# A hybrid decoder layer: FFN up-projection by seven Strassen products per value/gate pair, down-projection in groups of 4 k tiles between the pairs

## The reference, cut to what matters

```python
def conv_ffn(xn, buf, w_up, cw, cb, w_down):        # xn: 576 tokens used x 1024
    up = xn @ w_up                                   # 1024 x 5632: value half, gate half
    upc, new_buf = causal_dwconv(up, buf, cw, cb)    # width 3, along the tokens
    val, gate = jnp.split(upc, 2, axis=-1)
    return (jax.nn.gelu(gate) * val) @ w_down, new_buf   # 2816 x 1024

x = x + merged @ w_out
x = x + conv_ffn(rms_norm(x, norm2_g), ...)[0]
```

## Time and profile before

| | |
|---|---|
| median of 3 runs | 1052.52 us (1052.02 to 1055.92) |
| span of the profiled execution | 1050.4 us |
| mean granted TensorE clock | 0.997 |
| 19513 instructions, of them matmuls | 7952 |

### The profile page before, as it was taken

The page is one execution under the profiler, slowest core; times in us unless marked ns, Lnnn a source line. Parts: engine busy times, 40 slices in busy tenths (PEclk is TensorE's granted clock), DMA queues, the critical chain, the costliest instruction groups (busy, mean ns, idle before and its releaser), DMA issues.

```text
span 1050.4 us, 19513 instructions
## 1 busy us (share of the span) xinstructions
PE 1037.5 (99%) x7952; PEld 1015.8 (97%) x7952; DVE 697.8 (66%) x1046; ACT 403.3 (38%) x593; POOL 369.7 (35%) x178
## 2 busy tenths in 40 slices
PE   8999999999999999999999999999999999999996
PEld 7899999999999999999999999999999999999996
DVE  6787558946656477474735769999930289999423
ACT  7567786314434433432522343222221122222432
POOL 4333334342322223222133344333433333344430
PEclk9999999999999999999999999999999999999998
DMA  8533332468486786874552223223332222323355
GB/s 215 172 87 94 102 93 69 108 177 222 106 246 172 157 256 146 221 186 138 178 179 82 81 80 101 81 84 90 96 97 77 61 81 86 91 86 101 93 101 169
DMA packets 262748, 132.90 MB, mean 127 GB/s; under 512 B 82208, under 2 KB 256533, under 8 KB 262408
## 3 DMA queue, kind: packets, MB, share of 16 engines
q1 hardware_dynamic: 262454, 131.63, 45.7%
q10 hardware_dynamic: 210, 0.07, 0.0%
HBM read 104.17 MB, written 25.29 MB: 123 GB/s over the span
## 4 chain that ended last, share of the span: by engine, by line
PE 93%; issue 3%; DVE 1%; POOL 1%; ACT 0%; DMA 0%; DVEq 0%; SPq 0%; POOLq 0%; ACTq 0%
PE ring L2307 44%; PE ring L2717 23%; PE bank L2717 17%; PE bank L2549 2%; PE bank L2353 1%; POOL wlo L1029 1%; PE bank L2532 1%; PE bank L2629 1%; PE bank L2460 1%; PE bank L2617 1%; DMA x_tok<-in_x_prompt 0%; DVE x_split L1903 0%; PE ring L2340 0%; PE bank L2568 0%; PE bank L2588 0%
## 5 line engine op out<-in xcount | busy, mean ns | idle before, releaser
L2307 PE MATMUL ring<-x_split,whi 128*128 128x322 f32 (+2 forms) x1952 | 347.6, 300 | 0.1
L1029 POOL TENSOR_TENSOR wlo<-stage,whi 128x1024 fp32r<-128x1024 f32 x78 | 196.9, 2526 | 398.0 <-ACT whi L1088 398.0
L2307 PEld LDWEIGHTS ring<-x_split,whi 128*128 128x128 f32 x1952 | 294.5, 189 | 8.9 <-issue 8.1
L2307 PE MATMUL ring<-x_split,wlo 128*128 128x256 f32 (+1 forms) x976 | 210.4, 297 | 0.0
L2307 PEld LDWEIGHTS ring<-x_split,wlo 128*128 128x128 f32 x976 | 164.6, 189 | 0.0
L1088 ACT ACTIVATE whi<-stage 128x1024 fp32r<-128x1024 f32 x79 | 83.3, 1054 | 81.3 <-PE ring L2307 69.6
L1073 POOL TENSOR_TENSOR wlo<-stage,whi 128x1024 fp32r<-128x1024 f32 x28 | 71.8, 2565 | 108.1 <-ACT whi L1463 108.1
L2717 PE MATMUL ring<-x_split,whi 128*128 128x256 f32 (+1 forms) x512 | 88.7, 295 | 0.0
L1578 DVE SCALAR_TENSOR_TENSOR conv<-up,cols,conv 128x592 f32<-128x592 f32 x88 | 75.5, 858 | 3.1
L2717 PEld LDWEIGHTS ring<-x_split,whi 128*128 128x128 f32 x512 | 77.0, 189 | 0.0
L2208 DVE TENSOR_SCALAR conv<-up,cols 128x592 f32<-128x592 f32 x44 | 72.2, 1641 | 3.1
(11 more groups left out here) (403 smaller groups left out, 2112.6 us busy)
## 6 DMA issues: line engine op xcount, KB each, us to landing
stage<-in_w_in SPq DMA_DIRECT2D x56, 512.0 KB, 4.2
stage<-in_w_up SPq DMA_DIRECT2D x44, 512.0 KB, 3.8
stage<-in_w_down SPq DMA_DIRECT2D x16, 704.0 KB, 4.5
stage<-in_w_branch_a SPq DMA_DIRECT2D x8, 512.0 KB, 3.8
c_sample<-in_state_mlstm_C SPq DMA_DIRECT2D x16, 256.0 KB, 6.9
out_s_mlstm_C<-c_sample SPq DMA_DIRECT2D x16, 256.0 KB, 2.4
stage<-in_w_branch_b SPq DMA_DIRECT2D x8, 512.0 KB, 3.9
stage<-in_w_out SPq DMA_DIRECT2D x8, 512.0 KB, 3.7
```

Source lines behind the costliest of these rows:

```text
L1029: pool.tensor_tensor(spaced(wlo[:, slot]), packed(stage[:, slot, 0:n]), spaced(whi[:, slot]).bitcast(F32), ALU.subtract).then_inc(w_lo, 1)
L2307: last = pe.matmul(of(z, t0 or -2, t1), w[:, kk * WS:kk * WS + P], x_, start=kk == 0 and m == 0, stop=kk == kn - 1 and m == 2)
```

## The change

It does the up-projection of a value/gate pair as a 2 x 2 block product: blocks over the k halves (4 k tiles each), value and gate, and two token parts of 290 columns that overlap by two. Seven block products (`B11`, `B21`, `B22`, `T1` to `T4`) take the place of eight. Four of them (`T1`, `T2`, `T3`, `B22`) use sums of x blocks and four (`T1` to `T4`) sums of weight quarters; x sums are formed once, in the w_out stage, by ACT and DVE, and their high and low parts kept (`fxh`, `fxl`, seven operands); the weight sums are formed for each pair by DVE in place (`weight_sums`, `weight_sum_two`, `weight_sum_four`), 512 elements per partition each. Products that several results need are accumulated in one bank and copied out in between by ACT (`first_part`, `second_part`, `third_part`); DVE adds the copies to what is in PSUM and scales them into `up`.

A weight piece is now a quarter or a sum of quarters (512 elements) and goes through a ring of 7 slots of high and low parts; ACT rounds piece n + 7 after TensorE has used piece n, POOL subtracts. The first tap goes from DVE to ACT; the history copy becomes a max of an operand with itself.

The down-projection goes in groups of 4 k tiles (the last has 2), accumulated in `resid`: two of the 8 tiles of a group stand between the products of a pair, from pair 5 on; the last two groups come behind the pairs, in one accumulation. Evictions of down tiles rise from 16 to 40. Several semaphores that fire once are merged, and the last stores of the convolution's rows move behind the other stores.

```diff
+GROUP, LAG, GROUPS = 4, 5, 6
+RING = 7
...
+def down_at(i):
+    g, step = divmod(i - LAG, GROUP)
+    return (g, 2 * step) if 0 <= g < GROUPS - 2 and i < NPAIR else None
...
+def weight_order():
+    for i in range(NPAIR):
+        d = down_at(i)
+        yield "B11", i
+        yield "B21", i
+        if i:
+            yield "T4", i - 1
+        if d:
+            yield "D", *d
+        yield "T2", i
+        if i:
+            yield "B22", i - 1
+        yield "T1", i
+        if d:
+            yield "D", d[0], d[1] + 1
...
+        def down_out(g, m):
+            if g < GROUPS - 2:
+                return wide[1]
+            return (wide[1], bank2(0), wide[0], bank2(1))[m % 4 if m < 7 else 0]
...
+            def load_pair(i):
+                if i >= 2:
+                    sp.wait_ge(piece_split, split_done("B22", i - 2))
+                for q0, c0 in ((0, P * i), (2, FF + P * i)):
+                    sp.dma_start(fst[i % 2][:, q0:q0 + 2].rearrange("p q (k m) -> p (q k) m", m=P),
+                                 w_up.rearrange("(k p) m -> p k m", p=P)[:, :, c0:c0 + P]).then_inc(pair_loaded[i % 2], 16)
...
+            for n, key in enumerate(PIECES):
+                pool.wait_ge(piece_rounded, rounded(*key))
+                pool.tensor_tensor(in_blocks(flo[n % RING], key), packed(piece(key)),
+                                   in_blocks(fhi[n % RING], key).bitcast(F32), ALU.subtract).then_inc(piece_split, 1)
...
+                    act.wait_ge(t_done, 4 * i + SUM_AT[op])
+                else:
+                    act.wait_ge(pair_loaded[i % 2], pair_in(i))
+                if n >= RING:
+                    act.wait_ge(tile_done, unit_done(*PIECES[n - RING]))
+                act.activation(in_blocks(fhi[n % RING], key), packed(piece(key)), ACT.Copy).then_inc(piece_rounded, 1)
...
+            def ahead(*key):
+                if UNIT[key] + RING < len(PIECES):
+                    piece_hi(UNIT[key] + RING)
...
+            def first_tap(i, j):
+                ft = i + UPT // 2 * j
+                act.wait_ge(up_ready, 2 * i + j + 1)
+                if i:
+                    act.wait_ge(prod_done, i)
+                act.activation(cv[:, j, 0:CV_N], up[:, j, 0:CV_N], ACT.Identity,
+                               scale=cols[:, C_FCW[0] + ft:C_FCW[0] + ft + 1], bias=cols[:, C_FCB + ft:C_FCB + ft + 1]
+                               ).then_inc(tap_done, 1)
...
+            for i in range(NPAIR):
+                d = down_at(i)
+                first_part(i)
+                ahead("B11", i)
+                ahead("B21", i)
+                if i:
+                    ahead("T4", i - 1)
+                if i >= 2:
+                    product_hi(i - 2)
+                if d:
+                    ahead("D", *d)
+                second_part(i)
+                if i:
+                    first_tap(i - 1, 0)
+                ahead("T2", i)
+                if i:
+                    ahead("B22", i - 1)
+                ahead("T1", i)
+                if i:
+                    first_tap(i - 1, 1)
+                if d:
+                    ahead("D", d[0], d[1] + 1)
+                third_part(i)
+                ahead("T3", i)
+                if i:
+                    gelu(i - 1)
+            def square(m):
+                act.wait_ge(tile_evicted, down_out_count(FINAL + m + 1))
+                if m >= 3:
+                    act.wait_ge(fin_acc, m - 2)
...
+            def weight_sums(i):
+                dve.wait_ge(pair_loaded[i % 2], pair_in(i))
+                w = fst[i % 2]
+                tt(w[:, 4], w[:, 3], w[:, 2], ALU.subtract).then_inc(t_done, 1)
+                tt(w[:, 2], w[:, 2], w[:, 0], ALU.subtract).then_inc(t_done, 1)
+            def weight_sum_two(i):
+                w = fst[i % 2]
+                dve.wait_ge(t_done, 4 * i + 2)
+                dve.wait_ge(piece_split, split_done("B11", i))
+                tt(w[:, 0], w[:, 2], w[:, 3], ALU.subtract).then_inc(t_done, 1)
+            def weight_sum_four(i):
+                w = fst[i % 2]
+                dve.wait_ge(t_done, 4 * i + 3)
+                dve.wait_ge(piece_split, split_done("B21", i))
+                tt(w[:, 1], w[:, 1], w[:, 0], ALU.add).then_inc(t_done, 1)
...
+            def x_low(op, k, in_, f=None):
+                dve.wait_ge(x2_hi, x_count(op, k))
+                if f is None:
+                    tt(fxl[op][:, k], in_, fxh[op][:, k].bitcast(F32), ALU.subtract).then_inc(x2_lo, 1)
+                else:
+                    mul_add(fxl[op][:, k], in_, gain(f), fxh[op][:, k].bitcast(F32), ALU.mult, ALU.subtract).then_inc(x2_lo, 1)
...
+                if f < QK:
+                    tt(xdiff[:, :], one, two, ALU.subtract).then_inc(x2_sum, 1)
+                    x_low("B11", k_, one, f)
+                    x_low("T3", k_, xdiff[:, :], f)
+                else:
+                    n = QK + 3 * k_
+                    dve.wait_ge(x2_hi, x_count("T3", k_))
+                    mul_add(xsum[:, k_], two, gain(f), xsum[:, k_]).then_inc(x2_sum, 1)
+                    dve.wait_ge(x2_sum, n + 1)
+                    mul_add(xdiff[:, :], halves_of(k_)[0], gain(k_), xsum[:, k_], ALU.mult, ALU.subtract).then_inc(x2_sum, 1)
+                    dve.wait_ge(x2_sum, n + 2)
+                    mul_add(xfour[:, :], one, gain(f), xdiff[:, :]).then_inc(x2_sum, 1)
+                    x_low("B21", k_, one, f)
+                    x_low("T1", k_, xsum[:, k_])
+                    x_low("T2", k_, xdiff[:, :])
+                    x_low("T4", k_, two, f)
+                    dve.wait_ge(x2_sum, n + 3)
...
+            def last_rows(i, j):
...
+                ft, U = i + UPT // 2 * j, up[:, j]
+                h_ = hist[:, :, ft:ft + UPT + 1:UPT]
+                st(tt(sample_rows(U)[:, :, 0:FW - 1], h_, h_, ALU.max))
+                st.wait()
+                cpy(flast[:, ft].rearrange("p (b l) -> p b l", l=2),
+                    grouped(U[:, US0 - 2:UW_F - 2], UG)[:, :, 0:2]).then_inc(up_ready, 1)
...
+            def first_sum(i):
+                dve.wait_ge(part_copied, parts(i, 1))
+                dve.wait_ge(tile_done, unit_done("B21", i))
+                tt(s_one[:, 0:QS], s_one[:, 0:QS], acc(i, 1)[:, 0:QS], ALU.add).then_inc(c11_added, 1)
...
+            def third_scaled(i):
+                z = acc(i, 0)
+                dve.wait_ge(tile_done, unit_done("T4", i))
+                dve.wait_ge(c11_scaled, i + 1)
+                st(tt(up[:, 0, QS:US0], z[:, 0:UH_F], rtwo[:, 0:UH_F], ALU.mult))
+                tt(sample_rows(up[:, 0])[:, :, FW - 1:], grouped(z[:, UH_F:QT], LS), grouped(rtwo[:, UH_F:QT], LS), ALU.mult
+                   ).then_inc(c21_scaled, 1)
+                last_rows(i, 0)
+            def second_sum(i):
+                s_ = s_two[i % 2]
+                dve.wait_ge(part_copied, parts(i, 2))
+                dve.wait_ge(tile_done, unit_done("B22", i))
+                tt(s_[:, 0:QS], s_[:, 0:QS], acc(i, 2)[:, 0:QS], ALU.add).then_inc(c12_added, 1)
+                dve.wait_ge(c12_added, i + 1)
+                st(tt(up[:, 1, 0:QS], s_[:, 0:QS], rbc[:, 0:QS], ALU.mult))
+                last_rows(i, 1)
...
+            def fourth_sum(i):
+                dve.wait_ge(part_copied, parts(i, 3))
+                dve.wait_ge(tile_done, unit_done("T1", i))
+                tt(s_three[:, :], s_three[:, :], acc(i, 2)[:, 0:QT], ALU.add).then_inc(c22_added, 1)
...
+            def other_taps(i, j):
+                ft, U, c_ = i + UPT // 2 * j, up[:, j], cv[:, j, 0:CV_N]
+                w = [cols[:, C_FCW[m] + ft:C_FCW[m] + ft + 1] for m in range(FW)]
+                dve.wait_ge(tap_done, 2 * i + j + 1)
+                st.link(mul_add(c_, U[:, 1:1 + CV_N], w[1], c_))
+                ins = mul_add(c_, U[:, 2:2 + CV_N], w[2], c_)
...
+            def down_evict(g, m):
+                dve.wait_ge(tile_done, unit_done("D", g, m))
+                tt(resid[:, m, META:], of_down(down_out(g, m), META), resid[:, m, META:], ALU.add).then_inc(tile_evicted, 1)
+            for i in range(NPAIR):
+                d = down_at(i)
+                if i >= 2:
+                    product(i - 2)
+                if i:
+                    third_scaled(i - 1)
+                else:
...
+                first_sum(i)
+                if i >= 2:
+                    product_lo(i - 2)
+                if i + 1 < NPAIR:
+                    weight_sums(i + 1)
+                if i:
+                    other_taps(i - 1, 0)
+                first_scaled(i)
+                if i + 1 < NPAIR:
+                    weight_sum_two(i + 1)
+                if d:
+                    down_evict(*d)
+                if i:
+                    second_sum(i - 1)
+                if i + 1 < NPAIR:
+                    weight_sum_four(i + 1)
+                if i:
+                    other_taps(i - 1, 1)
+                if d:
+                    down_evict(d[0], d[1] + 1)
+                fourth_sum(i)
+            i = NPAIR - 1
...
```

(43 more changed lines are left out.)

805 lines of the change are left out of this document (431 added, 374 removed).

## The result

The changed kernel takes 1181.17 us (median of four runs, 1179.93 to 1185.31) against 1053.56 of the kernel before on the same chip: ratio 1.122, 95% interval 1.120 to 1.125. It is 12% slower. The profiled execution has a span of 1178.4 us.

A forecast was written before the change was run, and what follows sets the result against it. It took TensorE as the FFN's bound before, DVE and POOL's shared SBUF access after: start 642 + loop 474 + down work 28.3 + end 11.1 = span 1155.6, median 2.1 above, 1158 us; range 1085 to 1225.

The forecast's parts named there:

- TensorE's part: FFN matmuls: a product takes 1.59 us, a pair 11.13 instead of 12.72, 17.4 with down work; 22 pairs save 35 us.
- Price of a POOL piece: POOL's split of a 512-element weight piece takes 1.30 us; 9.1 us per pair, 11.7 with down pieces.
- DVE's own work: DVE's unblocked time in the FFN loop: 11.25 us per pair, 12.75 with down work.
- Who is blocked: DVE operations with both inputs in SBUF and POOL subtractions exclude each other; DVE operations with a PSUM input run free.
- How much of POOL's time falls on DVE: In the FFN loop 85% of POOL's time adds to DVE's: 19.0 us per pair, 22.7 with down work.
- rival (3): In the FFN loop POOL's short pieces find gaps better and overlap shortens DVE's list: 1095 us; chance 0.05.
- No wait of DVE in the loop's sum: DVE's loop is 474 us of its own and POOL's time; the load wait adds nothing, up to 2 us per pair.
- eviction ring: From first down tile's eviction through second down tile to DVE's third scaling: 9.5 us on TensorE, just closing within 22.7 us.
- rival (2): In the FFN TensorE waits some 5 us per pair and runs at 1.2 GHz for half of the ring: 1235 us; chance 0.12.
- Rival (1): In the FFN POOL and DVE run side by side without blocking, TensorE stays the bound: 1029 us; chance 0.10.
- Start and tail: DVE's loop starts at 642 us and ends at 1116; TensorE's remaining down work takes 28.3 us, the end 11.1.
- What would show it: Signs in the FFN: TensorE 85 to 90% busy, periods 21 to 24 us, DVE near 100%, no DMA wait.

The follow-up runs named there:

- write-only run: Changed kernel with POOL's subtractions for the FFN weights replaced by memsets of zero of about the same length, so POOL reads nothing: 1104.2 us.
- both orders changed: Changed kernel with the weight load released after T4's split, ScalarE's product high part made earlier, and the first down tile evicted ahead of the taps: 1124.56 us.
- low parts on DVE: Changed kernel with weight pieces' low parts in the loop subtracted by DVE instead of POOL: 1139.3 us alone, 1072.25 with earlier load and earlier eviction.

## Why the prediction was right, and where not

The direction and the size are right: 1158 forecast, range 1085 to 1225, measured 1181.2. But the 1158 came out near the result because two errors nearly cancelled, and that is luck. With the share of POOL's time that was measured, about 0.6, the forecast's own sum gives a loop of 268.8 + 241.8 x 0.6 = 414 us and a time of 1098 us (an estimate); the loop takes 494, and the 80 us between them are waits that the sum doesn't hold.

- **TensorE's part**: right. A product takes 1.60 to 1.64 us (forecast 1.59), a pair with down work 17.6 (17.4).
- **Price of a POOL piece**: right. 1.29 or 1.30 us unhindered (mean 1.47, with DVE in its way).
- **DVE's own work**: 12.35 and 10.76 us instead of 12.75 and 11.25. Right within 0.5.
- **Who is blocked**: right in kind, as the five rows of DVE's means and the write-only run show.
- **How much of POOL's time falls on DVE**: mis-sized. The step took 85%, read off one pair of the kernel before, from a copy and a tensor_scalar rather than from instructions with two SBUF inputs. Measured in the changed kernel: (19.24 - 12.35) / 11.7 = 59%, and (16.55 - 10.76) / 9.1 = 64% without down work; with both orders changed 61% and 69%. This is what rival (3) had said (1095, chance 0.05), and its price for it was about right. DVE's busy time of a pair is 19.2 us, not 22.7. In the run with both orders changed, where DVE is nearly full, the periods are 20.5 and 17.7 us where 22.7 and 19.0 were forecast.
- **No wait of DVE in the loop's sum**: the step that failed. DVE stands idle 4.7 us in a pair with down work. The forecast had priced the wait for the load at nothing up to 2 us; the load now takes 5.3 us instead of 3.8 and stands in the chain of waits in 14 of 15 periods. The eviction ring it had looked at in rival (2): 9.5 us of TensorE's work and 13.1 of DVE's, POOL's share included, close just in time for 22.7 us. In the period from 783.7 to 807.65 us TensorE's part is 12.2 us, since the waiting lowers the clock for the very tile in the ring (5.8 instead of 3.15 us), and DVE's part, from the third scaling at 795.97, is 11.6: 23.9 together. So the ring is 1.3 us longer than forecast, and the sum that it was compared with is 3.5 us shorter; the two are no longer alike, and the ring sets the period. 22.7 - 3.5 + 4.7 make 23.9.
- **Rival (2), the cold clock**: occurred in part. The clock is below full in the FFN, 0.89 from 640 to 1140 us, but holding it up gave back only 17.6 us. As worded (TensorE at half clock half of the time, 1235) it was too dear.
- **Rival (1), no blocking**: false, and not only because the blocking is real. With it gone the time is 1104, with loads and eviction out of the way too 1051, not 1029. The last of these lost most of the 35 us that TensorE saves, by its work in the windows shown under that run: the start costs 12.7 us (96 matmuls fewer by 640 us than in the kernel before; forecast 12); from 640 to 1000 a matmul takes 134.6 ns instead of 132.0, 7 us, and 2 us are idle; 5.4 us are lost from 1000 to the last matmul, 2.3 of them in the wait for the last pair's low part and 1.3 in that for the convolution's last rows; and the end takes 2.5 us more. Beyond the 12 us of start that the forecast had, that is 18 of the 22 us.
- **Start and tail**: the loop starts at 639.5 instead of 642, lasts 494 instead of 474 and ends at 1133.8. TensorE's last down work then takes 30.5 us (forecast 28.3; it stands idle 1.3 us of it until ScalarE has copied out the last convolution rows, `fc_evicted`, which the sum had left out), and from the last matmul (1164.4) to the end it is 14.0 instead of 11.1 us, since the reload of `y` (7.03 us from 1162.43 on) now lands after it. -2.5 + 20 + 5 = 23 over the forecast span.
- **What would show it**: TensorE 90% busy (forecast 85 to 90), a mean of the weight sums above 0.68 (1.27 for the first of the four, 0.97 over all), POOL's pieces near 1.3: as said. The period of 24.2 lies just over the forecast 21 to 24; "DVE near 100% busy from 642 on" was wrong (80% from 640 to 1140), and so was "no wait for DMA"; they are the two marks of the missing rings.

The order of causes, then. From the kernel before's side: nearly all of the change's TensorE saving is used up by its own start, drain and tail and by slightly longer matmuls (1051 against 1052.5). The turns of DVE and POOL cost up to 73 us on top, measured as 1124.6 - 1051.2 (this also holds what the loads cost once both orders are changed); 52 of them are won back with all the work kept, by low parts on DVE (1072.3). The two rings cost 57, measured as 1181.2 - 1124.6. What each ring costs alone can't be given: opened alone, load and high part gave 6, the eviction 38, both 57.

## What to carry to other kernels

A sum of busy times per period is only a lower bound. Where the same tile or buffer is handed round between engines (here a single PSUM output and a double-buffered weight load), write out each ring with its queued neighbours and with the prolonged durations, and compare its length with the sum; if two are alike, opening one can show little (6 us here), and only opening both tells. Then move the instruction that frees the single buffer ahead of the work it doesn't need: here one moved line was worth 38 us. And where DVE and POOL both read SBUF, a short POOL operation given to DVE can be a gain although DVE is the fuller engine.

## What the runs showed of the hardware

- POOL operations that only write (memset, 0.53 us for 512 elements) leave DVE's two-SBUF-input instructions at 0.684 us; subtractions of the same tiles draw them out to 1.27 us on average.
- Short DVE instructions are hit as hard as long ones in absolute time: a 64-wide multiplication of 0.219 us took 1.20 on average, the first weight sum cut to 8 elements 1.26 on average.
- Waiting costs TensorE twice. In the changed kernel it stood idle 2.7 to 5.4 us before the second down tile, and the 24 matmuls behind the wait took 4.7 to 6.1 us, with a granted clock of 0.55 in the one from 783.7 us, nearly all of it at the lower of the two levels (1.2 and 2.4 GHz); they take 3.15 to 3.5 at full clock. With 24 further matmuls in the place of the wait they took 3.5 in 14 of 16 pairs.
